# Spreading rms factors over the partitions: fp32 products of diagonals, or a row in DRAM and a broadcast

## The reference

```
def rms_norm_2(x, g):
    y = xf * lax.rsqrt(jnp.mean(xf * xf, axis=-1, keepdims=True) + RMS_EPS)
    return y * g

for layer in range(2):
    h = h + 0.5 * swiglu_ffn(rms_norm_2(h, ffn1_norm[layer]), ...)      # D_FF 2816
    u = rms_norm_2(h, mix_norm[layer])
    layer 0: h = h + conformer_conv(u, ...)                             # GLU, 31 taps, layer norm
    layer 1: h = h + stick_breaking_attention(u @ attn_w_q, k, v) @ attn_w_o
    h = h + 0.5 * swiglu_ffn(rms_norm_2(h, ffn2_norm[layer]), ...)
    after layer 0: k, v = split(rms_norm_2(h, kv_norm) @ w_kv)          # 16 heads of 64
return rms_norm_2(h, final_norm)
```

## Time and profile before

| | us |
|---|---|
| median of 3 runs | 1265.34 |
| the profiled execution | 1266.64 |
| its span, first to last instruction | 1264.9 |
| PE busy | 1255.5 |
| DVE busy | 827.1 |
| ACT busy | 619.9 |
| POOL busy | 85.1 |

### The profile page before, as it was taken

One profiled execution on the slowest core, in us unless ns is written; L12 is line 12 of the kernel. 1 busy time (PEld: TensorE's weight loads), 2 busy tenths in 40 slices (PEclk: granted clock), 3 DMA queues, 4 the chain that ended last, 5 costly groups with the idle time before them and its releaser, 6 DMA issues.

```text
span 1264.9 us, 16671 instructions
## 1 busy us (share of the span) xinstructions
PE 1255.5 (99%) x6814; PEld 1074.5 (85%) x6814; DVE 827.1 (65%) x953; ACT 619.9 (49%) x765; POOL 85.1 (7%) x122
## 2 busy tenths in 40 slices
PE   9999999999999999999999999999999999999998
PEld 7888877888988888879888889898888988988886
DVE  6565577667667656676777655656765666876653
ACT  5354566543555534444555543445553454555542
POOL 2223010101000002001000000000000110100000
PEclk9999999999999999999999999999999999999999
DMA  9654544456655566534565655656655513666640
GB/s 311 208 158 162 198 136 141 164 195 199 195 188 183 176 224 219 185 125 151 190 192 183 200 168 190 200 167 199 200 168 199 170 64 111 210 196 200 200 166 34
DMA packets 165388, 225.28 MB, mean 178 GB/s; under 512 B 7520, under 2 KB 106436, under 8 KB 165312
## 3 DMA queue, kind: packets, MB, share of 16 engines
q1 hardware_dynamic: 163488, 220.23, 53.3%
q0 software_dynamic: 1808, 3.98, 1.1%
q10 hardware_dynamic: 16, 0.00, 0.0%
HBM read 223.14 MB, written 1.05 MB: 177 GB/s over the span
## 4 chain that ended last, share of the span: by engine, by line
PE 97%; DVE 2%; ACT 1%; DMA 0%; issue 0%; SPq 0%; ACTq 0%
PE acc L680 15%; PE acc L621 15%; PE acc L623 15%; PE acc L622 15%; PE att L680 8%; PE acc L678 8%; PE att L678 4%; PE acc L654 2%; PE acc L658 2%; PE acc L656 2%; PE tp L701 1%; PE att L621 1%; PE att L623 1%; PE att L622 1%; DVE wlo L1550 1%; ACT whi L1174 0%
## 5 line engine op out<-in xcount | busy, mean ns | idle before, releaser
L1550 DVE TENSOR_TENSOR wlo<-raw,whi 128x2048 fp32r<-128x2048 f32 x205 | 467.7, 2289 | 165.4 <-ACT whi L1174 165.4
L1174 ACT ACTIVATE whi<-raw 128x2048 fp32r<-128x2048 f32 x205 | 388.6, 1912 | 92.8 <-PE acc L623 80.1
L680 PE MATMUL acc<-aT,whi 128*128 128x512 f32 x832 | 290.9, 391 | 0.0
L678 PE MATMUL acc<-aT,wlo 128*128 128x256 f32 x832 | 233.6, 281 | 0.0
L680 PEld LDWEIGHTS acc<-aT,whi 128*128 128x128 f32 x832 | 155.6, 187 | 33.8
L621 PE MATMUL acc<-whi,aT 128*128 128x512 f32 x432 | 172.9, 400 | 0.5 <-DVE wlo L1638 0.5
L623 PE MATMUL acc<-wlo,aT 128*128 128x512 f32 x432 | 168.9, 391 | 0.0
L622 PE MATMUL acc<-whi,aT 128*128 128x512 f32 x432 | 168.7, 391 | 0.0
L680 PE MATMUL att<-aT,whi 128*128 128x512 f32 x448 | 157.8, 391 | 0.0
L678 PEld LDWEIGHTS acc<-aT,wlo 128*128 128x128 f32 x832 | 157.3, 189 | 0.0
L621 PE MATMUL acc<-whi,hT_hi 128*128 128x512 f32 x348 | 135.7, 390 | 0.0
(11 more groups left out here) (332 smaller groups left out, 1588.1 us busy)
## 6 DMA issues: line engine op xcount, KB each, us to landing
raw<-in_ffn_w_gate_dram SPq DMA_DIRECT2D x88, 512.0 KB, 4.0
raw<-in_ffn_w_up_dram SPq DMA_DIRECT2D x88, 512.0 KB, 5.1
raw<-in_ffn_w_down_dram SPq DMA_DIRECT2D x88, 512.0 KB, 4.8
raw<-in_w_in_dram SPq DMA_DIRECT2D x70, 512.0 KB, 4.8
raw<-in_conv_w_pw_dram SPq DMA_DIRECT2D x24, 512.0 KB, 4.9
raw<-in_w_kv_dram SPq DMA_DIRECT2D x16, 512.0 KB, 5.0
raw<-in_ret_w_o_dram SPq DMA_DIRECT2D x8, 512.0 KB, 4.3
raw<-in_diff_w_o_dram SPq DMA_DIRECT2D x8, 512.0 KB, 4.2
```

Source lines behind the costliest of these rows:

```text
L678: mm_(bank[:, 0:T], wlo[:, slot, cols], aT_hi[:, kt, :], start=half == 0 and j == 0, stop=False, skip_group_check=True)
L680: last = mm_(bank[:, :], whi[:, slot, cols], aT[:, kt, :, :].rearrange("p a n -> p (a n)"), start=False, stop=half == 1 and j == SLAB_K - ...
L1174: A_(whi[:, slot, :], raw[:, slot, :], ACT.Copy).then_inc(hi_ready, 1)
L1550: V.tensor_tensor(wlo[:, slot, :], raw[:, slot, :], whi[:, slot, :].bitcast(F32), ALU.subtract)\
```

## The change

The diagonals, the products with them and the copies go. Behind each rs that is spread, GpSimd issues two DMAs of 128 single words each into a row of 256 in DRAM, halves rs as before, waits for both DMAs, and issues a DMA that reads the row onto all 128 partitions of `rsb`. VectorE's `rs_rows` waits for its landing, at the place where it copied. TensorE keeps a product of ones by 32 columns of ones behind slab 2 of each of the four FFNs. The product at L734 stays. The tile `rdiag` is gone, and the tiles behind it move by 1 KB.

```diff
-        rdiag = sb("rdiag", [P, TT, P], to=second)
...
-        rdiag_ready = sem("rms_diagonal_ready"); rsb_mm = sem("rms_spread"); rsb_ready = sem("rms_rows_ready")
+        rs_written = sem("rms_row_written"); rsb_ready = sem("rms_rows_ready")
...
+        SPREAD_USES = [RS_F1A, RS_F2A, RS_KV, RS_MIXB, RS_F2B]
+        rs_row = nc.dram_tensor("rms_rows", (len(SPREADS), T), F32, kind="Internal").ap()
...
                 pool.wait_ge(rs_ready, use + 1)
+                if use in SPREAD_USES:
+                    n = SPREAD_USES.index(use)
+                    for t in range(TT):
+                        pool.dma_start(rs_row[n, t * P:(t + 1) * P].rearrange("(p a) -> p a", a=1),
+                                       rs[:, use, t:t + 1]).then_inc(rs_written, 16)
                 nc.gpsimd.tensor_scalar(rs_down[:, use, :], rs[:, use, :], 0.5, None, ALU.mult)\
                     .then_inc(rs_down_ready, 1)
+                if use in SPREAD_USES:
+                    pool.wait_ge(rs_written, 32 * (n + 1))
+                    pool.dma_start(rsb[:, :], rs_row[n:n + 1, :].to_broadcast([P, T])).then_inc(rsb_ready, 16)
...
-                if name == "ffn1b":
-                    pe.wait_ge(rsb_ready, SPREADS.index("kv") + 1)
...
-                    if s == 2 and name in SPREADS:
-                        spread_rs(name, tp[0])
-                    elif s == 2:
-                        for _ in range(TT):
-                            mm_(tp[0][:, 0:P], ones[:, :], ones[:, :], start=True, stop=True)
+                    if s == 2:
+                        if name == "ffn1a":
+                            pe.wait_ge(pool_ready, 3)
+                        mm_(tp[0][:, 0:32], ones[:, :], ones[:, 0:32], start=True, stop=True)
...
-                if s == 2:
-                    spread_rs("kv", att[0])
...
-            spread_rs("q", att[0])
...
-            def rs_rows(name, bank):
-                n = SPREADS.index(name) + 1
-                dve.wait_ge(rsb_mm, n)
-                V.tensor_copy(rsb[:, :], bank[:, 0:T]).then_inc(rsb_ready, 1)
-                dve.wait_ge(rsb_ready, n)
+            def rs_rows(name):
+
+                dve.wait_ge(rsb_ready, 16 * (SPREADS.index(name) + 1))
...
-                if name in SPREADS:
-                    diagonal(use)
```

More of the change, by code:

```diff
@@ L683, in wide_slab @@
                     last.then_inc(half_done, 1)
[L685 to L693, removed]
             def fill(b, src, kts):
@@ L775, in ffn_pe @@
                     if s == 6 and name != "ffn2b":
-                        if name in SPREADS:
-                            pe.wait_ge(rsb_ready, SPREADS.index(name) + 1)
                         exit_fills(w.b, w.g + FC, 0)
@@ L1887, in ffn_dve @@
                 low(w.k + 1 + AHEAD)
-                if name in SPREADS:
-                    diagonal(use)
                 low(w.k + 2 + AHEAD)
                 if name in SPREADS:
-                    rs_rows(name, tp[0])
+                    rs_rows(name)
                 summed(0)
@@ L2061, in _ @@
                     kept_lo(pkv.b, 0, "ffn1b")
-                if s == 2:
-                    diagonal(RS_KV)
                 if s == 3:
-                    rs_rows("kv", att[0])
+                    rs_rows("kv")
                 if s in (3, 4):
@@ L2080, in _ @@
                     exit_lo(pq.b - 2, 1, "mixb")
-                if s == 2:
-                    diagonal(RS_MIXB)
                 if s == 3:
-                    rs_rows("q", att[0])
+                    rs_rows("q")
                     turned_out(qT[:, 0:4, :], pq.g, lambda bank: dve.wait_ge(half_done, 2 * pq.k + 4 + bank),
```

## The result

The changed kernel takes 1296.65 us (median of 5 runs, 1294.86 to 1296.76) against 1265.52 (1265.23 to 1265.79) for the kernel before in the same comparison: a ratio of 1.0239, 95% interval 1.0228 to 1.025. That is 31 us slower, where 2.2 us faster was forecast, and outside the range. The profiled execution took 1295.11 us, its span is 1293.4 against 1264.9: 28.5 us more, to be found in the rows.

The account below looks back on a forecast made before the run. TensorE was taken to bound the kernel (busy 1255.5 of 1264.9 us). Removing 2.70 us of products and adding 0.48 gave 2.2 less, with no stall: 1265.34 - 2.2 = 1263.1 us, range 1262.3 to 1265.9.

Parts of the forecast that it names:

- the middle one: At five spread sites, GpSimd's trip through DRAM was set against each site's room; no stall forecast, at 63%.
- c: Time from the end of the power at L485 to the broadcast's landing: 10.8 us, between 7.7 and 16.9.
- The rooms: Longest c costing nothing: q 11.4, ffn2b 13.0, ffn1a 15.7 us; ffn2a and kv more than ffn2b.
- rival 1: Late round trip at q, ffn2b, ffn1a: (c - 11.4) + (c - 13.0) + (c - 15.7), positive parts; c over 14.6: 6%.
- The price of a stall: At q, each microsecond of c above the room was to cost one microsecond.
- The slots: On TensorE: 2.70 us of products removed, four 32-column products at 0.12 added (0.48), net 2.2 us less.
- Covered work: VectorE's removed diagonals and copies (4.9 us), slab-load sharing and GpSimd's later constants were to change nothing.
- The figure of the Trainium skill: GpSimd DMA at about 2.0 us fixed plus bytes over 436 GB/s, making c about 5 us; prediction followed the trace.
- Rival 2: At q, GpSimd's broadcast issue waits for VectorE's low parts: 0.7 to 2.9 us stall; within the 19% small-stall case.
- Rival 3: Wide-slab pace hangs on the preceding fp32 product: 1216 pairs 0.01 us slower, 12 us; 6%, and 6% faster.
- Rival 4: TensorE's modelled ends hide a wait taking the 2.2 us back: 1265.3; only the upper edge of the 63%.

Follow-up runs that it names:

- E4: Kernel before plus nine GpSimd DMAs at three idle places (words side by side, 512 bytes apart, pairs, and others), which only GpSimd waits for: 1265.41 us.
- E10: Changed kernel, trips unchanged, with the factors in each FFN first used behind chunk 1's gate and up sums: 1274.62 us, ratio 1.007.
- E1: Changed kernel, but broadcasts land in an unread tile and VectorE uses ones, waiting for rs itself; rms factor left out: 1263.93 us, ratio 0.9986.
- E5: Changed kernel with one DMA write of 128 pairs instead of two of words; VectorE takes the landed row apart: 1276.63 us, ratio 1.0083.
- E2: E1 without the 32-column product of ones behind slab 2 of the FFNs: 1270.96 us, ratio 1.0042.
- E3: Kernel before without the two unread fp32 products of ones in ffn1b's slab 2: 1267.16 us, ratio 1.0011.
- E9: Kernel before with each spread, and ffn1b's products of ones, done by two fp32r products; VectorE splits the diagonals: 1272.18 us, ratio 1.0053.
- E7: Kernel before with one 32-column product behind slab 4 of ffn1b in place of the two behind slab 2: 1266.71 us in one run.

## Why the prediction was wrong

The step that failed is the middle one, the length of the trip against its room, in both of its numbers.

- **c.** Predicted 10.8 us, bounds 7.7 to 16.9; measured 17.2 to 18.6, outside the bounds. The part up to the broadcast's issue was to be 5.4 and is 10.9 at q (1014.62 to 1025.47); the broadcast was to be 5.4 and is 6.4 to 7.1. The wrong term is the landing of the second word write, 4.5 predicted and 9.0 to 10.5 measured, sized by reads of words into SBUF and by SP's store of long rows: E4 has such reads at 4.5 and such rows at 4.2 also, and words side by side to DRAM at 9.8. The two writes also land one after the other, 2.8 to 4.5 us apart. The text named it ("a write of 128 words to DRAM by GpSimd is in no row") and then gave it no wider bound than its neighbours had.
- **The rooms.** q's 11.4 was right: late by 5.8, a gap of the same size. For the FFNs only the bank of slab 4's first half was followed; the low part behind the wait was called looser. It leads through ScalarE's cast to the gate sum that the second half of slab 4 needs, and that one comes first: 13.3, 12.4 and 10.6 instead of 15.7, more than 13.0, and 13.0. "ffn2a and kv have more room than ffn2b" was true, but ffn2a's 12.4 was as far from enough as the others, and kv's 17.0 fell short as well. With c as measured and the rooms as predicted, rival 1's formula gives 12.9 us; the missed deadlines add 11.9 (late by 24.8 in all). E10, which moves the use and not the trip, shows both at once.
- **The price of a stall.** One us per us was assumed. q's stall of 5.8 cost 8.0, since TensorE comes back at a granted clock of 0.63, and ffn1a and ffn2b kept a slower pace for the rest of the FFN, 1.9 us each.
- **The slots.** 2.70 us removed was right. The 32-column product costs 0.23, not 0.12: the upper bound. The lower one came from L1116's products, which have another shape. The saving is 1.8 (E1), not 2.2; on its own this would have missed by 0.4.
- **Covered work.** Right: VectorE's 4.9 us gave nothing, and the DMA traffic cost nothing that shows (E1). No product waited for GpSimd's constants either, but ones was set at 327.26 and not at about 323, 0.5 us ahead of the product at 327.98 that needs it.
- **The figure of the Trainium skill.** The estimate of c that the prediction worked out from the Trainium skill (DMA: Bandwidth & Descriptors, Anatomy of one DMA), about 5 us, is off by more than three times for this trip; and none of E4's landings was under 3.0 us, where it puts a small one at about 2.0.
- **Rivals.** Rival 1, at 6%, is what happened, above its own upper end, since that end was made of the same neighbouring rows. Rival 2 did not: L496 issued in 537 to 641 ns, two of them beside a low part, and L502 in 584 to 592, though with VectorE idle; E5's broadcast at q was issued beside low parts (1014.63) and took 0.59 us. What waited was GpSimd's halving at 1104.34, beside the low part of 1103.53 to 1105.82: 1.56 us instead of 0.24, to 1105.90. Rival 3's condition did not arise at the product (32 columns suffice), but its mechanism is real (E2, E3, E9) at 0.0066 us a pair, not 0.01: 1216 x 0.0066 is 8.0 us. It came into the loss through the stalls. Rival 4 did not: E1 has the slots back.
- **Two slips in its sums.** At a c of 14.6 rival 1's formula gives 1267.9, not 1267.7, and the range's upper end of 1265.9 belongs to a c of 13.6, not near 14. Neither matters for what happened.

What stays open: why ffn2a kept its pace behind a stall in the changed kernel and ffn2b did in E5, while others lost it; why the clock fell behind ffn2a's gaps in E5 (1.40 and 2.45 us) and not behind ffn2b's (1.98 and 2.48); and what in the write of neighbouring words takes the time.

## What to carry to other kernels

When work off the bounding engine is replaced by a longer trip, follow every instruction that stands behind the new wait, through the other engines' queues, to the point where the bounding engine needs its result: the second deadline can be earlier than the first. An operation that no row shows gets bounds as wide as its unlikeness, and where the rooms are within a microsecond or two of the estimate, the change is a bet on that one landing. Moving the first use of a late result was cheaper here than making the result early: the same trips that cost 22 us in the FFNs cost nothing when the scaling stood some 6 us further behind rs (E10).

## What the runs showed of the hardware

- Single words written by GpSimd side by side into DRAM landed in 8.0 to 10.4 us alone and in up to 12.6 behind another such write; 512 bytes apart in 5.7 to 6.5; as pairs in 5.2 to 8.3 (E4, E5).
- A stream of alternating 256- and 512-column products of the fast 4-byte kind (fp32r) has two spacings at one and the same granted clock of 1.00, 0.347 and 0.353 us a pair (233 or 228 starts in 40 us). With an fp32 product between the 256-column slabs and the first of these it is the shorter, without one the longer, and a later product doesn't change it (E2, E3, E7, E9). Behind a stall it can change too: it did in ffn1a and ffn2b of the changed kernel, not in ffn2a.
- An fp32 product with 32 moving columns holds TensorE as long as one with 128: 0.23 against 0.22 us.
- Behind a stall of 5.8 us TensorE's granted clock was 0.63 over 6 us, and the stall cost 8.0.
- A broadcast of a 1 KB row from DRAM to 128 partitions landed in 3.2 to 3.4 us with the DMA engines' share at 0.32 to 0.46 (E4), and in 6.4 to 7.1 at 0.81 to 0.90 (the changed kernel).
- GpSimd's issues of DMAs took no longer beside VectorE's low parts (0.54 to 0.64 us, the changed kernel and E5), but a small tensor_scalar of GpSimd beside one took 1.56 us instead of 0.24 and ended 0.1 us behind it.
